# Two of 42 weight slabs multiplied without a split, and the finished output scattered without one, in the small slots of a mixture-of-experts kernel

## The chip, the cores and the metric

The kernel runs on one core of one Trainium2 chip. The metric is the device time of one execution in microseconds (us); smaller is better. The time before is the median of three runs.

## The reference

Two layers of a hybrid mixer with a residual each, the first followed by a dense SwiGLU, the second by a mixture of experts. Only the mixture of experts bears on the change:

```python
SEQ, D_MODEL, N_EXPERTS, TOP_K, D_FF_EXPERT = 256, 1024, 8, 2, 3584

def swiglu(h, w_gate_up, w_down):
    gt, up = jnp.split(h @ w_gate_up, 2, axis=-1)
    return (jax.nn.silu(gt) * up) @ w_down

def moe_swiglu(h, w_router, w_gate_up, w_down):
    t = h.reshape(-1, dm)                                   # 256 x 1024
    top_val, top_idx = lax.top_k(t @ w_router, TOP_K)
    combine = jnp.sum(jax.nn.one_hot(top_idx, N_EXPERTS) * jax.nn.softmax(top_val)[..., None], axis=1)
    y = jnp.zeros_like(t)
    for e in range(N_EXPERTS):
        y = y + combine[:, e:e + 1] * swiglu(t, w_gate_up[e], w_down[e])
    return y
```

All of it is float32: an expert has 1024 x 7168 weights for gate and up and 3584 x 1024 for down, 44 MB.

## The kernel before

**Split precision.** TensorE multiplies in a reduced form of float32 (`F32R`). So a matrix is split into a high part, `hi`, the operand rounded to `F32R`, and a low part, `lo = x - hi`. ScalarE writes the high part and VectorE the low part. A product is then three matmuls: hi x hi, hi x lo, lo x hi.

**Slots.** The expert stage works in slots `i`. A slot gathers up to 128 tokens of one expert (a full slot), or up to 64 (a small slot, `few`). Slots 2, 4 and 6 are small, all others full; eight slots, 0 to 7, are run with these inputs. In a small slot the stationary operand holds the high part of 64 tokens in its columns 0 to 63 and their low part in columns 64 to 127, so that two matmuls for each piece of weight, with `exp_hi` and with `exp_lo` (L2308, L2309), give all four terms. The rows of the low part are then added to the others by `fold_low`: ScalarE copies the product to `low_part` (L1163) and TensorE adds it through the matrix `fold`.

**Slabs.** Each slot streams the 44 MB of its expert from HBM in 42 slabs of 1 MB, 128 x 2048. SyncE issues their transfers (L572) into 14 buffers, `exp_slots`: slab `j` is asked for once TensorE has used slab `j - 14` (semaphore `slab_used`). ScalarE writes `exp_hi[:, place, :]` (L1121), a ring of `EXP_RING` = 6 places; VectorE writes the low part over the raw slab (L1671), since `exp_lo` and the raw buffers are the same memory. The function `ring_plan` says which place slab `j` takes and which slab, its `holder`, was there before. Both engines put their splits into their own program with `expert_split(i, few, used)`, called each time the program passes one more slab of TensorE's: it writes out further splits until

```python
place, holder = RINGS[few][j]
if holder >= used - LATE:        # LATE = 1
    return
```

so the number of splits that stand ahead of any other instruction of ScalarE or VectorE is fixed by the holders.

**A slot's order.** The hidden width 3584 is done in `STEPS` = 4 steps of 1024, 1024, 1024 and 512 columns. Step `s` makes the gate in PSUM bank pair 0 (`block(0, s, ..)`), the up product in pair 1 (`block(1, s, ..)`), and then the down product of the step before, `down(s - 1, ..)`. In slabs: step 0 has 0 to 7; step 1 has 8 to 11 (gate), 12 to 15 (up) and 16 to 19 (down); step 2 has 20 to 31 in the same way; step 3 has 32 and 33 (gate), 34 and 35 (up); then come 36 to 41 (down). ScalarE takes the silu of the gate (L1172), VectorE multiplies with the up product in `hidden(s)` (L1803), TensorE transposes the result in `turn_hidden(s)` (L2337), and ScalarE and VectorE split it (L1179, L1812).

**The two places.** In a small slot TensorE cannot begin slab 12, which overwrites bank pair 1, before `hidden(0)` has read that pair (place 1, behind slab 11); and it cannot run `turn_hidden(2)` before `hidden(2)` (place 2, behind slab 33).

**The finished output.** At the start of slot `i` the result of slot `i - 1` is copied from PSUM to `ysp[:, 0, :]` by ScalarE (L1190), its low part is made by VectorE in `output_lo` (L1770), and TensorE scatters both to the token rows by eight matmuls with the 0/1 matrix `selT` (`scatter`, L2075) behind slab 3. VectorE adds them to `xs` in `add_slot` (L1778).

Each engine runs its own program in order; semaphores alone connect them.

Of the kernel before, what the change touches and what calls it, by code (L numbers as in the profile page):

```python
# [22 lines left out]
F32 = mybir.dt.float32  # L23
# [34 lines left out]
EXP_RAW, EXP_RING, LATE = 14, 6, 1  # L58
# [12 lines left out]
EXP_SLABS = sum(2 * a + b for a, b in zip(GU, DN))  # L71
HT = DM // P
HT_END = STEP[-1][1] // P
assert EXP_SLABS % EXP_RAW == 0
UNSPLIT = ()


def ring_plan(few):

    plan, holders = [], [n - EXP_RING for n in range(EXP_RING)]  # L80
    for j in range(EXP_SLABS):
        if few and j in UNSPLIT:
            plan.append(None)
            continue
        place = sum(x is not None for x in plan) % EXP_RING
        plan.append((place, holders[place]))
        holders[place] = j
    assert holders == [EXP_SLABS - EXP_RING + n for n in range(EXP_RING)]
    return plan


RINGS = {few: ring_plan(few) for few in (False, True)}


def column(n):
# [98 lines left out]
def trunk(nc, x_in, mem_in, mix_norm_g, w_in, sb_q_g, sb_k_g, gla_a_up, gla_a_b, gla_o_g, ca_q_g,  # L194
# [5 lines left out]
    PRE = len(flat)  # L200
# [4 lines left out]
    with ExitStack() as ctx:  # L205
# [58 lines left out]
        exp_hi = sb("exp_hi", [P, EXP_RING, EXP_SLAB], F32R)  # L264
# [70 lines left out]
        count, key, rank, cap, few = (sm(240 + 8 * i, E) for i in range(5))  # L335
# [6 lines left out]
        pa = ctx.enter_context(nc.psum_tensor("pa", [P, 4 * BW], F32))  # L342
# [489 lines left out]
        def _(act):  # L832
# [277 lines left out]
            def expert_split(i, few, used, at_most=EXP_SLABS):  # L1110

                nonlocal j
                while j < at_most:
                    if RINGS[few][j] is not None:
                        place, holder = RINGS[few][j]
                        if holder >= used - LATE:
                            return
                        act.wait_ge(more_ready[j % EXP_RAW], i * (16 * EXP_SLABS // EXP_RAW)
                                    + 16 * (j // EXP_RAW + 1))
                        act.wait_ge(slab_used, i * EXP_SLABS + (PRE + holder + 1))  # L1120
                        act.activation(exp_hi[:, place, :], exp_slots[j % EXP_RAW], ACT.Copy)\  # L1121
                            .then_inc(hi_ready, counted(few, j))
                    j += 1
# [23 lines left out]
            def expert(i, few, next_few, folds=0):  # L1147
# [93 lines left out]
        def _(dve):  # L1241
# [541 lines left out]
            def expert(i, few, next_few, folds=0):  # L1783
# [111 lines left out]
        def _(pe):  # L1895
# [178 lines left out]
            def mm(dst, a, b, start, stop):  # L2074
                return pe.matmul(dst, a, b, start=start, stop=stop, skip_group_check=True)  # L2075
# [194 lines left out]
            def find_tokens(n):  # L2270
# [3 lines left out]
                    ins = mm(ps[:, DM:DM + 2], sel[:, t, :], token_no[:, t, :], t == 0, t == NT - 1)  # L2274
                ins.then_inc(token_found, 1)

            def scatter(n, halves=1):


                pe.wait_ge(selt_ready, n)  # L2280
                pe.wait_ge(y_lo, n + (halves - 1))
                for t in range(NT):
                    for c in range(2):
                        for h in range(2):
                            dst = (1 - t) * DM + c * BW
# [12 lines left out]

            def expert(i, few, folds=0):
                at = i * EXP_SLABS  # L2300
                j = 0

                def terms(dst, src, k, cols, first, last):

                    m_hi, m_lo = exp_hi[:, RINGS[few][j][0], cols], exp_lo[j % EXP_RAW][:, cols]
                    if not few:
                        return passes(dst, src[:, 0, k, :], src[:, 1, k, :], m_hi, m_lo, first, last)
                    pe.matmul(dst, src[:, 0, k, :], m_hi, start=first, stop=False)  # L2308
                    return pe.matmul(dst, src[:, 0, k, :], m_lo, start=False, stop=last)  # L2309
# [64 lines left out]
                for s in range(STEPS):  # L2374
# [81 lines left out]
```

## Time and profile before

| | us |
|---|---|
| median of 3 runs (1696.69 to 1698.57) | 1698.41 |
| the profiled execution's own time | 1697.4 |
| its span | 1695.5 |
| TensorE busy in the span | 1624.8 |
| VectorE busy | 1305.0 |
| ScalarE busy | 1107.4 |

The expert stage fills the second half. The copies L1190 that open slots 1 to 7 begin at 894.78, 1015.65, 1120.51, 1239.49, 1343.79, 1462.67 and 1567.64 us, and the last engine stops at 1695.5. Between two of these copies lies one slot. In the lists of this document an instruction stands with the time at which it begins, its duration, its engine, its line and operation, what it writes and what it reads; in square brackets stands how long the engine was idle before it, and what it waited for. TensorE's matmuls overlap in their pipeline: what a matmul takes away from the engine is the distance from its start to that of the next, not its duration, and the same holds to a smaller extent for VectorE and ScalarE.

### The profile page before, as it was taken

How to read it: one execution, taken by the hardware profiler on the slowest of the kernel's cores; microseconds unless marked ns; L12 is line 12 of the kernel's file. 1: busy time of each engine (PE TensorE's matmuls, PEld its weight loads, DVE VectorE, ACT ScalarE, POOL GpSimd, SP SyncE). 2: the span in 40 equal slices, each digit the busy share in tenths (PEclk: the TensorE clock that was granted, in tenths of full speed). 3: DMA queues.
4: the chain of work that ended last, by engine and by line, in shares of the span. 5: the costliest groups of instructions: out<-in, count | busy, mean ns of one | idle time of the engine just before them, and what ended most of it. 6: DMA issues, size and time to landing. Idle time of an engine off the chain costs nothing.

```text
span 1695.5 us, 20153 instructions
## 1 busy us (share of the span) xinstructions
PE 1624.8 (96%) x7598; PEld 1331.5 (79%) x7598; DVE 1305.0 (77%) x968; ACT 1107.4 (65%) x950; POOL 111.0 (7%) x123
## 2 busy tenths in 40 slices
PE   7999998999999999999999998899989899988998
PEld 5777886888887778877788887688877788876886
DVE  6654666555666546658989889999899998999985
ACT  5557554444555475546677778887689777887773
POOL 4111000000011110000400000000000000000000
PEclk9999999999999999999999999999999999999999
DMA  7554544656566544479999999999999999999990
GB/s 274 174 148 141 157 146 157 210 177 199 166 216 175 140 148 149 149 292 374 339 370 371 378 367 393 404 409 405 398 385 398 409 409 401 385 397 409 409 387 25
DMA packets 161335, 484.84 MB, mean 286 GB/s; under 512 B 12992, under 2 KB 15072, under 8 KB 161248
## 3 DMA queue, kind: packets, MB, share of 16 engines
q1 hardware_dynamic: 158112, 474.16, 76.9%
q0 software_dynamic: 3136, 9.48, 1.6%
q8 instruction: 60, 0.98, 0.2%
q14 instruction: 27, 0.22, 0.0%
HBM read 481.50 MB, written 2.10 MB: 285 GB/s over the span
## 4 chain that ended last, share of the span: by engine, by line
PE 81%; DVE 12%; issue 3%; ACT 2%; POOL 1%; DMA 0%; DVEq 0%; POOLq 0%; ACTq 0%
PE pa L1971 18%; PE pa L1973 17%; PE pa L1972 17%; DVE exp_lo_a L1671 5%; PE ps L2075 5%; PE ps L1971 4%; PE ps L1973 4%; PE ps L1972 4%; PE pa L2308 3%; PE pa L2309 3%; DVE exp_lo_b L1671 2%; PE ps L2337 1%; PE ps L2308 1%; PE ps L2309 1%; POOL hrs L712 1%
## 5 line engine op out<-in xcount | busy, mean ns | idle before, releaser
L1671 DVE TENSOR_TENSOR exp_lo_a<-exp_raw_a,exp_hi 128x2048 fp32r<-128x2048 f32 x240 | 538.4, 2288 | 28.9 <-ACT exp_hi L1121 28.5
L1121 ACT ACTIVATE exp_hi<-exp_raw_a 128x2048 fp32r<-128x2048 f32 x240 | 451.7, 1920 | 80.2 <-PE pa L1973 39.2
L1257 DVE TENSOR_TENSOR w_lo<-w_raw,w_hi 128x1024 fp32r<-128x1024 f32 (+1 forms) x228 | 277.2, 1231 | 136.2 <-ACT w_hi L846 127.1
L846 ACT ACTIVATE w_hi<-w_raw 128x1024 fp32r<-128x1024 f32 (+1 forms) x228 | 236.9, 1054 | 171.4 <-PE pa L1973 147.7
L1971 PE MATMUL pa<-w_hi,r 128*128 128x512 f32 x600 | 240.2, 400 | 0.0
L1973 PE MATMUL pa<-w_hi,r 128*128 128x512 f32 x600 | 234.2, 390 | 0.0
L1972 PE MATMUL pa<-w_lo,r 128*128 128x512 f32 x600 | 234.0, 390 | 0.0
L1671 DVE TENSOR_TENSOR exp_lo_b<-exp_raw_b,exp_hi 128x2048 fp32r<-128x2048 f32 x96 | 217.8, 2289 | 14.5 <-ACT exp_hi L1121 13.6
L1971 PE MATMUL pa<-exp_hi,xg 128*128 128x512 f32 x560 | 220.2, 393 | 2.5 <-ACT xg L1133 1.5
L1973 PE MATMUL pa<-exp_hi,xg 128*128 128x512 f32 x560 | 218.3, 390 | 0.0
L1121 ACT ACTIVATE exp_hi<-exp_raw_b 128x2048 fp32r<-128x2048 f32 x96 | 182.7, 1919 | 30.7 <-PE pa L1973 22.7
L2308 PE MATMUL pa<-exp_hi,xg 128*128 128x512 f32 x336 | 139.2, 414 | 14.3 <-issue 14.2
L1972 PE MATMUL pa<-exp_lo_a,xg 128*128 128x512 f32 x380 | 148.0, 389 | 0.0
L1971 PE MATMUL pa<-w_hi,xt 128*128 128x512 f32 (+1 forms) x320 | 124.5, 389 | 9.4 <-DVE xt L1293 9.4
L1971 PEld LDWEIGHTS pa<-w_hi,r 128*128 128x128 f32 x600 | 112.7, 188 | 25.5 <-issue 2.0
L1973 PEld LDWEIGHTS pa<-w_hi,r 128*128 128x128 f32 x600 | 112.7, 188 | 24.3
L1972 PEld LDWEIGHTS pa<-w_lo,r 128*128 128x128 f32 x600 | 112.8, 188 | 21.9
L1971 PEld LDWEIGHTS pa<-exp_hi,xg 128*128 128x128 f32 x560 | 105.2, 188 | 24.5 <-ACT xg L1133 1.6
L1973 PE MATMUL pa<-w_hi,xt 128*128 128x512 f32 (+1 forms) x320 | 122.9, 384 | 0.0
L1972 PE MATMUL pa<-w_lo,xt 128*128 128x512 f32 (+1 forms) x320 | 122.9, 384 | 0.0
L1973 PEld LDWEIGHTS pa<-exp_hi,xg 128*128 128x128 f32 x560 | 105.1, 188 | 22.1
L1971 PE MATMUL ps<-exp_hi,hts 128*128 128x512 f32 x240 | 94.5, 394 | 0.0
(301 smaller groups left out, 2270.2 us busy)
## 6 DMA issues: line engine op xcount, KB each, us to landing
exp_raw_a<-in_moe_w_gate_up SPq DMA_DIRECT2D x152, 1024.0 KB, 9.9
exp_raw_a<-in_moe_w_down SPq DMA_DIRECT2D x88, 1024.0 KB, 8.6
exp_raw_b<-in_moe_w_gate_up SPq DMA_DIRECT2D x72, 1024.0 KB, 9.2
w_raw<-in_w_in SPq DMA_DIRECT2D x104, 512.0 KB, 4.2
exp_raw_b<-in_moe_w_down SPq DMA_DIRECT2D x24, 1024.0 KB, 8.3
w_raw<-in_ff_w_gate_up SPq DMA_DIRECT2D x44, 512.0 KB, 4.5
w_raw<-in_ff_w_down SPq DMA_DIRECT2D x22, 512.0 KB, 3.9
w_raw<-in_w_mem_kv SPq DMA_DIRECT2D x16, 512.0 KB, 5.8
```

The costliest lines, as they stand in the source:

```text
L712: pool.tensor_tensor(dst[:, 0:n], src[:, 0:n], half[:, 0:n], ALU.pow)\
L846: act.activation(w_hi[:, s % SPLIT, 0:n], raw_slot(s)[:, 0:n], ACT.Copy)\
L1121: act.activation(exp_hi[:, place, :], exp_slots[j % EXP_RAW], ACT.Copy)\
L1257: dve.tensor_tensor(w_lo[:, s % SPLIT, 0:w], raw_slot(s)[:, 0:w], w_hi[:, s % SPLIT, 0:w].bitcast(F32), ALU.subtract)\
L1671: dve.tensor_tensor(exp_lo[j % EXP_RAW], exp_slots[j % EXP_RAW], exp_hi[:, place, :].bitcast(F32), ALU.subtract)\
L1971: pe.matmul(dst, hi, m_hi, start=first, stop=False)
L1972: pe.matmul(dst, hi, m_lo, start=False, stop=False)
L1973: return pe.matmul(dst, lo, m_hi, start=False, stop=last)
L2075: return pe.matmul(dst, a, b, start=start, stop=stop, skip_group_check=True)
L2308: pe.matmul(dst, src[:, 0, k, :], m_hi, start=first, stop=False)
L2309: return pe.matmul(dst, src[:, 0, k, :], m_lo, start=False, stop=last)
L2337: ins = pe.transpose(dst[:, a * P:(a + 1) * P], hs[:, a * P:(a + 1) * P], ident[:, :])
```

## The change

In small slots slabs 11 and 33 are no longer split. TensorE multiplies them from the raw buffer with full float32 operands, in four matmuls in place of eight, and waits for the transfer itself (`more_ready`). ScalarE and VectorE leave them out, and so the holders of the slabs behind them change: six slabs behind each of them have holder `j - 7` in place of `j - 6`. The places of the ring are turned by two after each small slot (`ring_of`). The output of the full slot before is copied to `y_whole`, in the memory of `hts`, and scattered by four full float32 matmuls in place of eight; VectorE's `output_lo` is left out at the start of small slots. Full slots keep their instructions.

```diff
-UNSPLIT = ()
+UNSPLIT = (11, 33)
-def ring_plan(few):
-    plan, holders = [], [n - EXP_RING for n in range(EXP_RING)]
+def ring_plan(few, offset):
+    plan, holders = [], [(n - offset) % EXP_RING - EXP_RING for n in range(EXP_RING)]
     for j in range(EXP_SLABS):
         if few and j in UNSPLIT:
             plan.append(None)
             continue
-        place = sum(x is not None for x in plan) % EXP_RING
+        place = (offset + sum(x is not None for x in plan)) % EXP_RING
         plan.append((place, holders[place]))
         holders[place] = j
+def ring_of(i, few):
+    smaller = (i - 1) // 2 if type(i) is int and i > 0 else 0
+    return ring_plan(few, -smaller * len(UNSPLIT) % EXP_RING)
...
                     act.wait_ge(slab_used, at + PRE)
-                    act.activation(ysp[:, 0, :], ps[:, 0:DM], ACT.Copy).then_inc(y_hi, 1)
+                    act.activation(y_whole[:, :] if few else ysp[:, 0, :], ps[:, 0:DM], ACT.Copy)\
+                        .then_inc(y_hi, 1)
...
                     expert_split(i, few, 0)
-                    output_lo(i)
+                    if few:
+                        dve.sem_inc(y_lo, 1)
+                    else:
+                        output_lo(i)
...
+            def scatter_whole(n):
+                pe.wait_ge(selt_ready, n)
+                pe.wait_ge(y_hi, n)
+                for t in range(NT):
+                    for c in range(2):
+                        dst = (1 - t) * DM + c * BW
+                        ins = mm(ps[:, dst:dst + BW], selT[:, t * P:(t + 1) * P].bitcast(F32),
+                                 y_whole[:, c * BW:(c + 1) * BW], True, True)
+                    ins.then_inc(scattered, 1)
...
-                        pe.wait_ge(lo_ready, at + (PRE + j + 1))
+                        if ring[j] is None:
+                            pe.wait_ge(more_ready[j % EXP_RAW], i * (16 * EXP_SLABS // EXP_RAW)
+                                       + 16 * (j // EXP_RAW + 1))
+                        else:
+                            pe.wait_ge(lo_ready, at + (PRE + j + 1))
...
+                                if ring[j] is None:
+                                    ins = pe.matmul(dst, xg[:, 0, k, :].bitcast(F32),
+                                                    exp_slots[j % EXP_RAW][:, cols],
+                                                    start=k == 0, stop=k == KT - 1)
+                                else:
+                                    ins = terms(dst, xg, k, cols, k == 0, k == KT - 1)
...
-                    if s == 0 and not is_first(i):
+                    if s == 0 and few:
+                        scatter_whole(i)
+                    elif s == 0 and not is_first(i):
                         scatter(i)
```

VectorE's program, from the start of small slot 2 to the split of the first hidden tile (L1812), before. L1770 is `output_lo`, L1778 `add_slot`, L1803 `hidden(0)`, L1671 the splits of slabs 5 to 18:

```order
L1770 TENSOR_TENSOR hts<-ps,hts 128x1024
L1671 TENSOR_TENSOR exp_lo_a<-exp_raw_a,exp_hi 128x2048 x2
L1671 TENSOR_TENSOR exp_lo_b<-exp_raw_b,exp_hi 128x2048
L1671 TENSOR_TENSOR exp_lo_a<-exp_raw_a,exp_hi 128x2048
L1778 SCALAR_TENSOR_TENSOR xs<-ps,small,xs 128x1024 x2
L1671 TENSOR_TENSOR exp_lo_a<-exp_raw_a,exp_hi 128x2048 x2
L1671 TENSOR_TENSOR exp_lo_b<-exp_raw_b,exp_hi 128x2048 x3
L1671 TENSOR_TENSOR exp_lo_a<-exp_raw_a,exp_hi 128x2048
L1803 TENSOR_TENSOR hs<-pa,hs 128x1024
L1819 TENSOR_SCALAR sel<-rev_tri,small 128x128 x2
L1671 TENSOR_TENSOR exp_lo_a<-exp_raw_a,exp_hi 128x2048 x4
L1812 TENSOR_TENSOR hts<-ps,hts 128x8x64
```

The same place now. The split is L1680, `add_slot` L1787, `hidden(0)` L1812, and the split of the hidden tile L1821; the first row holds the splits of slabs 0 to 6:

```order
L1680 TENSOR_TENSOR exp_lo_a<-exp_raw_a,exp_hi 128x2048 x7
L1680 TENSOR_TENSOR exp_lo_b<-exp_raw_b,exp_hi 128x2048
L1680 TENSOR_TENSOR exp_lo_a<-exp_raw_a,exp_hi 128x2048
L1787 SCALAR_TENSOR_TENSOR xs<-ps,small,xs 128x1024 x2
L1680 TENSOR_TENSOR exp_lo_a<-exp_raw_a,exp_hi 128x2048 x2
L1680 TENSOR_TENSOR exp_lo_b<-exp_raw_b,exp_hi 128x2048 x2
L1680 TENSOR_TENSOR exp_lo_a<-exp_raw_a,exp_hi 128x2048 x2
L1812 TENSOR_TENSOR hs<-pa,hs 128x1024
L1828 TENSOR_SCALAR sel<-rev_tri,small 128x128 x2
L1680 TENSOR_TENSOR exp_lo_a<-exp_raw_a,exp_hi 128x2048 x3
L1821 TENSOR_TENSOR hts<-ps,hts 128x8x64
```

`output_lo` is gone. Between `add_slot` and `hidden(0)` stand six splits before and now: slab 11 is missing, and slab 15 has moved ahead of `hidden(0)` in its stead. Behind `hidden(0)` three splits stand where four stood.

VectorE's program around `hidden(2)`, before. The first rows are eight splits, ending with slab 36; the last two rows of L1671 are slabs 37 and 38, then 39 and 40:

```order
L1671 TENSOR_TENSOR exp_lo_a<-exp_raw_a,exp_hi 128x2048 x6
L1671 TENSOR_TENSOR exp_lo_b<-exp_raw_b,exp_hi 128x2048
L1671 TENSOR_TENSOR exp_lo_a<-exp_raw_a,exp_hi 128x2048
L1803 TENSOR_TENSOR hs<-pa,hs 128x1024
L1671 TENSOR_TENSOR exp_lo_a<-exp_raw_a,exp_hi 128x2048 x2
L1812 TENSOR_TENSOR hts<-ps,hts 128x8x64
L1671 TENSOR_TENSOR exp_lo_b<-exp_raw_b,exp_hi 128x2048 x2
L1803 TENSOR_TENSOR hs<-pa,hs 128x512
```

The same place now; `hidden(2)` is the first L1812:

```order
L1680 TENSOR_TENSOR exp_lo_a<-exp_raw_a,exp_hi 128x2048 x5
L1680 TENSOR_TENSOR exp_lo_b<-exp_raw_b,exp_hi 128x2048
L1680 TENSOR_TENSOR exp_lo_a<-exp_raw_a,exp_hi 128x2048 x2
L1812 TENSOR_TENSOR hs<-pa,hs 128x1024
L1680 TENSOR_TENSOR exp_lo_a<-exp_raw_a,exp_hi 128x2048
L1680 TENSOR_TENSOR exp_lo_b<-exp_raw_b,exp_hi 128x2048
L1821 TENSOR_TENSOR hts<-ps,hts 128x8x64
L1680 TENSOR_TENSOR exp_lo_b<-exp_raw_b,exp_hi 128x2048
L1812 TENSOR_TENSOR hs<-pa,hs 128x512
```

Eight splits stand ahead of `hidden(2)` before and now: slab 33 is missing and slab 37 has moved ahead. One split fewer stands between the split of the hidden tile and `hidden(3)`.

TensorE's program at place 2, now: the last pair of slab 32, slab 33 from the raw buffer, `turn_hidden(2)`, and slab 34.

```order
L2332 MATMUL pa<-exp_hi,xg 128x512
L2333 MATMUL pa<-exp_lo_a,xg 128x512
L2351 MATMUL pa<-exp_raw_a,xg 128x512 x4
L2371 MATMUL ps<-ident,hs 128x128 x8
L2332 MATMUL pa<-exp_hi,xg 128x512
```

Before, four pairs of L2308 and L2309 stood where the four matmuls L2351 stand; the rest of the order is the same.

## Rows read from the trace of the kernel before

**Rows 1.** All engines' busy time in slots 2, 3, 4 and 6 (us).

```profile
core 0: us, PE busy (x) PEld busy (x) DVE busy (x) ACT busy (x) POOL busy (x), PEclk, DMA share, GB/s
...
1015.60:1120.50 104.90, 94.26 (x411) 76.14 (x410) 102.81 (x58) 89.97 (x61) 0.99 (x1) 0.93 1.02 401
1120.50:1239.50 119.00, 119.00 (x547) 98.86 (x546) 108.09 (x58) 87.67 (x55) 2.21 (x1) 1.00 1.02 397
1239.50:1343.80 104.30, 93.65 (x410) 75.71 (x409) 102.59 (x58) 89.97 (x62) 0.99 (x1) 0.95 1.02 402
...
1462.70:1567.60 104.90, 94.32 (x410) 76.19 (x409) 102.72 (x58) 89.91 (x61) 0.99 (x1) 0.93 1.02 403
```

**Rows 2.** TensorE in slot 2, in order of time.

```profile
1039.95 0.39 PE L2309 MATMUL pa<-exp_lo_b,xg 128*128 128x512 f32 x1
1045.08 0.76 PE L2308 MATMUL pa<-exp_hi,xg 128*128 128x512 f32 x1 [4.73 <-issue]
...
1090.07 0.39 PE L2308 MATMUL pa<-exp_hi,xg 128*128 128x512 f32 x1
1090.29 0.39 PE L2309 MATMUL pa<-exp_lo_a,xg 128*128 128x512 f32 x1
...
1098.45 1.97 PE L2337 MATMUL ps<-ident,hs 128*128 128x128 f32 x8 [5.61 <-DVE hs L1803]
```

**Rows 3.** VectorE in slot 2, in order of time.

```profile
1018.23 1.22 DVE L1770 TENSOR_TENSOR hts<-ps,hts 128x1024 fp32r<-128x1024 f32 x1
1019.36 4.48 DVE L1671 TENSOR_TENSOR exp_lo_a<-exp_raw_a,exp_hi 128x2048 fp32r<-128x2048 f32 x2
...
1041.56 2.28 DVE L1671 TENSOR_TENSOR exp_lo_a<-exp_raw_a,exp_hi 128x2048 fp32r<-128x2048 f32 x1
1043.76 1.22 DVE L1803 TENSOR_TENSOR hs<-pa,hs 128x1024 f32<-128x1024 f32 x1
...
1054.09 0.68 DVE L1812 TENSOR_TENSOR hts<-ps,hts 128x512 fp32r<-128x512 f32 x1
1055.62 4.49 DVE L1671 TENSOR_TENSOR exp_lo_a<-exp_raw_a,exp_hi 128x2048 fp32r<-128x2048 f32 x2 [0.85 <-ACT exp_hi L1121]
...
1097.17 1.23 DVE L1803 TENSOR_TENSOR hs<-pa,hs 128x1024 f32<-128x1024 f32 x1
```

**Rows 4.** Busy time in stretches of slots 2, 4 and 6; columns as in rows 1.

```profile
1015.60:1040.30 24.70, 24.70 (x111) 20.12 (x109) 24.70 (x14) 24.36 (x17) 0.00 (x0) 1.00 1.02 407
1040.30:1045.10 4.80, 0.07 (x2) 0.05 (x1) 4.80 (x5) 4.23 (x3) 0.00 (x0) 0.72 1.03 410
1045.10:1052.00 6.90, 6.90 (x27) 5.61 (x27) 6.90 (x6) 1.92 (x1) 0.00 (x0) 0.70 1.02 398
1052.00:1092.80 40.80, 40.49 (x181) 31.91 (x179) 39.92 (x22) 40.52 (x27) 0.99 (x1) 1.00 1.02 391
1092.80:1098.50 5.70, 0.10 (x2) 0.05 (x1) 5.70 (x5) 1.65 (x2) 0.00 (x0) 0.87 1.02 408
1098.50:1120.50 22.00, 22.00 (x96) 18.41 (x97) 20.79 (x13) 17.29 (x13) 0.00 (x0) 0.88 1.03 409
1323.00:1343.80 20.80, 20.80 (x96) 17.56 (x97) 20.63 (x13) 17.31 (x14) 0.00 (x0) 0.94 1.03 409
1545.60:1567.60 22.00, 22.00 (x96) 18.40 (x97) 20.76 (x13) 17.26 (x13) 0.00 (x0) 0.88 1.03 409
```

**Rows 5.** TensorE: eight full float32 matmuls of 256 columns (16 records), in order of time.

```profile
218.90 3.62 PE L2075 MATMUL ps<-ckT,cqT 128*128 128x256 f32 x16
222.16 0.58 PE L1971 MATMUL pa<-w_hi,r 128*128 128x512 f32 x1
```

**Rows 6.** ScalarE in slot 2, in order of time.

```profile
1053.68 3.72 ACT L1121 ACTIVATE exp_hi<-exp_raw_a 128x2048 fp32r<-128x2048 f32 x2
```

**Rows 7.** Transfer of slab 38: issue, us to landing, and ScalarE's splits 37 and 38.

```profile
1074.83 0.98 SPq L572 DMA_DIRECT2D exp_raw_a<-in_moe_w_down  x1
...
exp_raw_a<-in_moe_w_down SPq DMA_DIRECT2D x1, 1024.0 KB, 14.7
...
1090.21 3.75 ACT L1121 ACTIVATE exp_hi<-exp_raw_a 128x2048 fp32r<-128x2048 f32 x2
```

More of the change, by code:

```diff
@@ L84, in ring_plan @@
             continue
-        place = sum(x is not None for x in plan) % EXP_RING
+        place = (offset + sum(x is not None for x in plan)) % EXP_RING
         plan.append((place, holders[place]))
         holders[place] = j
-    assert holders == [EXP_SLABS - EXP_RING + n for n in range(EXP_RING)]
+    assert sorted(holders) == [EXP_SLABS - EXP_RING + n for n in range(EXP_RING)]
     return plan
-RINGS = {few: ring_plan(few) for few in (False, True)}
+def ring_of(i, few):
+    smaller = (i - 1) // 2 if type(i) is int and i > 0 else 0
+    return ring_plan(few, -smaller * len(UNSPLIT) % EXP_RING)
+assert 3 * len(UNSPLIT) % EXP_RING == 0 and EXP_SLABS % EXP_RING == 0
 def column(n):
@@ L103, in counted @@
 def counted(few, j):
-    return 2 if j + 1 < EXP_SLABS and RINGS[few][j + 1] is None else 1
+    return 2 if few and j + 1 in UNSPLIT else 1
 CAP, FEW = P, P // 2
@@ L270, in trunk @@
         with nc.sbuf_tensor("route_x", [P, NT, KT, P], F32) as route_x:
+            pass
+        with nc.sbuf_tensor("y_whole", [P, DM], F32) as y_whole:
             pass
@@ L1113, in expert_split @@
                 while j < at_most:
-                    if RINGS[few][j] is not None:
-                        place, holder = RINGS[few][j]
+                    if ring_of(i, few)[j] is not None:
+                        place, holder = ring_of(i, few)[j]
                         if holder >= used - LATE:
@@ L1665, in expert_split @@
                 while j < at_most:
-                    if RINGS[few][j] is not None:
-                        place, holder = RINGS[few][j]
+                    if ring_of(i, few)[j] is not None:
+                        place, holder = ring_of(i, few)[j]
                         if holder >= used - LATE:
@@ L2300, in expert @@
                 at = i * EXP_SLABS
+                ring = ring_of(i, few)
                 j = 0
                 def terms(dst, src, k, cols, first, last):
-                    m_hi, m_lo = exp_hi[:, RINGS[few][j][0], cols], exp_lo[j % EXP_RAW][:, cols]
+                    m_hi, m_lo = exp_hi[:, ring[j][0], cols], exp_lo[j % EXP_RAW][:, cols]
                     if not few:
@@ L2319, in block @@
                             for c in range(0, w, BW):
-                                ins = terms(pa[:, bank * DM + c:bank * DM + c + BW], xg, k,
-                                            slice(kk * w + c, kk * w + c + BW), k == 0, k == KT - 1)
+                                dst = pa[:, bank * DM + c:bank * DM + c + BW]
+                                cols = slice(kk * w + c, kk * w + c + BW)
+                                if ring[j] is None:
[4 more added lines that the diff above has]
+                                    ins = terms(dst, xg, k, cols, k == 0, k == KT - 1)
                         ins.then_inc(slab_used, 1)
```

## The prediction

> **What bounds the kernel now.** I read three views in turn: the engines' busy time slot by slot, TensorE in order of time inside a small slot, and VectorE beside it.
>
> The first [rows 1] separates the slots. In full slot 3 TensorE is busy for 119.00 of 119.00 us: it is the bound, and the change leaves its work there alone. In small slots 2, 4 and 6 TensorE has 94 us of work in 104.9, 104.3 and 104.9 us, while VectorE is busy for 102.8. The clock column shows 0.93 to 0.95 there against 1.00. The transfers move 397 to 403 GB/s in slots of both kinds, with a share of 1.02: they too have hardly anything to spare.
>
> TensorE's list shows where it stops [rows 2]. It issues the last matmul of slab 11 at 1039.95 and the next at 1045.08, after 4.73 us (place 1); the end of that wait has no releaser in the profile ("issue"), but `hidden(0)` ends at 1043.76 + 1.22 = 1044.98 [rows 3]. It stops again for 5.61 us until 1098.45, by name for VectorE's L1803, `hidden(2)` (place 2). Everything else is close: in 1015.6 to 1040.3 TensorE is busy for all 24.70 us, and from 1098.5 to the slot's end for all 22.00, with the next full slot behind it [rows 1, 4]. VectorE is busy for 24.70 of 24.70 and 4.80 of 4.80 us before place 1, and its one gap up to place 2 that I find is 0.85 us at 1055.62, where it waits for ScalarE's split [rows 3, 4].
>
> So a small slot is a relay: TensorE runs to place 1, VectorE decides when it goes on; VectorE decides again at place 2; from there to the end of the next full slot TensorE runs without a stop. **What a small slot saves is the time by which `hidden(2)` ends sooner, plus what TensorE's clock gains behind it.** Work taken off VectorE behind `hidden(2)` is worth nothing.
>
> The clock matters. During the wait at place 1 the granted clock falls from 1.00 (2.4 GHz) towards 0.5 (1.2 GHz), and in the 6.9 us behind it the mean is 0.70: 0.30 x 6.9 = 2.07 us lost. Behind place 2 the means are 0.88 over 22.0 us, 0.94 over 20.8 and 0.88 over 22.0 in the three small slots: 2.64, 1.25 and 2.64 us lost, 6.5 in all [rows 4].
>
> **The change, part by part, in slot 2.**
>
> *VectorE, `output_lo`.* L1770 begins at 1018.23 and the next split at 1019.36: 1.13 us go [rows 3]. VectorE does not pause from there to `hidden(0)`, so `hidden(0)` comes 1.13 us sooner.
>
> *VectorE, slab 11.* A split takes 1043.76 - 1041.56 = 2.20 us of the engine [rows 3]. The order printed above decides where this counts: ahead of `hidden(0)` stand as many splits as before, slab 15 in place of 11. Nothing is saved at place 1. Behind `hidden(0)` there is one fewer: 2.20 us sooner from L1812 on.
>
> *VectorE, slab 33.* Again as many splits, eight, stand ahead of `hidden(2)`; the one saved lies behind it, where TensorE is the bound. Worth 0; should TensorE not be the bound there, it would be 2.20 us.
>
> *TensorE, full precision.* No row shows a full float32 matmul with 512 columns. The nearest has 256: eight of them take 222.16 - 218.90 = 3.26 us, 0.41 us each [rows 5], so 0.82 for 512 and 3.3 us for four. The other end is four times a reduced matmul: 111 matmuls in 24.70 us are 0.225 us each [rows 4], hence 0.90 and 3.6 us. Eight reduced ones are 1.8 us. Each of the three replacements (scatter, slab 11, slab 33) therefore costs TensorE 1.5 us, at most 1.8. I take 1.5, since its row has the same kind of operand. The Trainium skill, "FP8 and Floating Point Precision", section "TensorE Precision Notes", has true FP32 as four passes through the array; by it the price would be the upper end, 1.8 us (the row of 256 columns shows 3.6 times a reduced matmul, a little less), and the forecast the same, for the reason that follows.
>
> *TensorE at place 1.* It would have been able to go on at 1039.95 + 0.225 = 1040.18; with 1.5 for the scatter and 1.5 for slab 11 that is 1043.2 (1043.8 by the upper end). `hidden(0)` lets it go at 1045.08 - 1.13 = 1043.95. So the extra work lies in the wait, of which 0.1 to 0.8 us stays. In 1052.0 to 1092.8 TensorE also pauses, for 0.31 us in all, and the clock stays at 1.00 [rows 4], so I take 1.00 behind place 1, and the 2.07 us come back: at what was 1052.0, TensorE is 1.13 + 2.07 = 3.2 us ahead. If the clock falls all the same, it is 1.13.
>
> *VectorE behind place 1.* By its own work it is 1.13 + 2.20 = 3.33 us ahead at L1812, and it has the gap of 0.85 us behind it. That gap ends with ScalarE's split of slab 19, which starts at 1053.68 [rows 6] behind the copy of TensorE's transposes, so it moves with TensorE, 3.2 us. Hence the next splits, and 41.5 us on, `hidden(2)`, come 3.2 us sooner. VectorE is busy for 39.92 of 40.8 us in that stretch [rows 4], and the same instructions stand in it.
>
> *TensorE at place 2.* Slab 32 ended at 1090.29 + 0.23 = 1090.5 and now ends at 1087.3, since it is paced by VectorE's splits. Slab 33 takes 3.3 us instead of 1.8 and needs no split: ready at 1090.6. `hidden(2)` lets it go at 1098.45 - 3.2 = 1095.25. TensorE still waits some 4.6 us, as long as at place 1 before, where the clock fell. So I leave the clock's loss behind place 2 as it is.
>
> *ScalarE* loses two splits and gains nothing; it waits for TensorE, not the reverse. *Other costs.* TensorE's wait for a transfer is met long before: slab 38, the tightest that I found, landed at 1074.83 + 14.7 = 1089.5, with ScalarE's split of it, the second of a pair from 1090.21, beginning near 1092.0 [rows 7].
>
> **Sum.** 3.2 us for each of three small slots: 9.6. Full slots 0. From the profiled execution's own 1697.4 that is 1687.8. The median of the runs lies 1.0 above that execution, so I predict **1688.8 us**.
>
> **The rivals.**
>
> *A. The clock holds at place 2.* The wait shrinks from 5.6 to 4.6 us, and where and how far the clock falls varies between slots already (0.94 against 0.88). If it stayed at 1.00 in all three, 6.5 us more would come back: 9.6 + 6.5 = 16.1, 1682.3 us. Against it: waits of 4.7 us at place 1 did bring it down [rows 4]. The other way, if it falls as long after the last matmul and for as long as now, 1.0 us less of the slow stretch lies in the wait: 0.5 us more is lost in each slot, and 1.4 more if slot 4 becomes like the others: 2.9 us less, 1691.7. The Trainium skill, "TensorE: Matmul & The Clock Gate", section "HAM oscillation — how this bites in real kernels", warns that waits of PE can make the clock fall anew each time round a loop; the rows of both places agree, and by it place 2 keeps its loss, as forecast.
>
> *B. The transfers become the bound.* A slab of 1.049 MB at 409 GB/s [rows 4] takes 2.56 us, 42 take 107.7, more than a small slot lasts; small and full slot together have 223.9 us for 215.4. After the change 220.7 are left, which still holds. But slab 38 had only 2.5 us to spare, less than 3.2: ScalarE would wait 0.7 us there. VectorE reaches that slab behind `hidden(2)`, so this is hidden. If the lag piles up from slot to slot, the later two small slots win nothing: 3.2 in all, 1695.2 us.
>
> *C. Slower: full precision costs more than the wait at place 1.* With x us for a full float32 matmul TensorE reaches place 1 at 1040.18 - 3.6 + 8x. Since the clock would not have fallen, it is later than before only beyond 1045.08 + 2.07 = 1047.15, x = 1.32. With 0.82 to 0.90 there is 3.4 us of room. It is passed if these matmuls run at half clock: x = 1.64 to 1.8 gives 1049.7 to 1051, 2.5 to 3.8 us later than before in each slot, 1706 to 1710 us. Against it: the clock is 1.00 up to place 1, and nothing ahead of it stops TensorE.
>
> *D. Place 1's clock still falls.* TensorE would gain only 1.13 us there and reach `turn_hidden(0)` that late, VectorE's gap would grow by 2.1 us, and the slot would save 1.1: 3.4 in all, 1695.0 us.
>
> **How the numbers follow.** Forecast 0.62, A's better half 0.16, B 0.08, D 0.08, C 0.06. A measurement of this kernel can tell about 0.2%, 3.4 us. The forecast and A are faster by more; B and D, at 3.2 to 3.4, stand at the border, half of them in each; the forecast's own tail and part of C give the rest. Faster 0.85, within 0.2% 0.10, slower 0.05. The likeliest case alone spans 1686 to 1691.7; with A below and B and D above I give 1682.5 to 1695.2.
>
> **What would show it.** Right: L1190 to L1190 in small slots near 101.5 us, full slots still 119; TensorE's wait at place 1 under 1 us with clock 1.00 behind it; the wait at place 2 near 4.6 us; each full-precision slab 3.3 to 3.6 us. Wrong: a `hidden(2)` that is not 3.2 us sooner (then a gap of VectorE ahead of it shows which engine it waits for), a small slot's last stretch shorter than 21 us at clock 1.00 (A), ScalarE waiting for transfers (B), or four matmuls of a raw slab above 5.3 us (C).

## The result, and the profile after

| | before | after |
|---|---|---|
| median of 5 runs (us) | 1697.39 (1696.69 to 1698.57) | 1687.55 (1686.59 to 1688.85) |
| ratio, 95% interval | | 0.994 (0.9927 to 0.9953) |
| profiled execution, its span | 1697.4, 1695.5 | 1686.59, 1684.8 |

The kernel became 9.8 us faster; 9.6 was forecast. The forecast time, 1688.8 us, holds 1.0 us that was added because the median of the first three runs lay above the profiled execution; over the five runs it does not (1697.39 against 1697.4). The copies that open slots 2 to 7 now begin at 1014.34, 1115.51, 1234.48, 1336.59, 1455.49 and 1556.44 us. The busy time of slots 2, 3, 4 and 6, and of the stretches behind the two places (columns as in rows 1; they answer to [rows 1, 4]):

```profile
1014.30:1115.50 101.20, 95.94 (x411) 74.07 (x410) 97.32 (x55) 86.99 (x59) 0.99 (x1) 0.98 1.02 401
1115.50:1234.50 119.00, 119.00 (x547) 98.85 (x546) 108.13 (x58) 87.67 (x55) 2.22 (x1) 1.00 1.03 406
1234.50:1336.60 102.10, 96.89 (x410) 74.86 (x409) 97.32 (x55) 87.07 (x60) 0.99 (x1) 0.97 1.03 405
1455.50:1556.40 100.90, 95.67 (x410) 73.94 (x409) 97.25 (x55) 86.91 (x59) 0.99 (x1) 0.98 1.02 402
...
1042.90:1049.80 6.90, 6.87 (x34) 5.82 (x35) 6.90 (x6) 3.95 (x5) 0.00 (x0) 1.00 1.02 407
1094.40:1115.50 21.10, 21.10 (x96) 17.70 (x97) 18.58 (x12) 15.49 (x12) 0.00 (x0) 0.92 1.03 409
1315.50:1336.60 21.10, 21.10 (x93) 17.53 (x92) 17.63 (x12) 15.52 (x13) 0.00 (x0) 0.89 1.03 409
1535.50:1556.40 20.90, 20.86 (x96) 17.61 (x97) 18.63 (x12) 15.46 (x12) 0.00 (x0) 0.93 1.03 409
```

The full slot is as long as before, 119.0 us. The small slots went from 104.9, 104.3 and 104.9 to 101.2, 102.1 and 100.9. Behind place 1 the clock is 1.00 where it was 0.70. Behind place 2 it still falls.

TensorE in slot 2, in order of time (answers to [rows 2]): the scatter, slab 11, the restart at place 1, slab 33, the restart at place 2.

```profile
1021.39 3.60 PE L2087 MATMUL ps<-y_whole,selT 128*128 128x512 f32 x8
1024.42 0.79 PE L2332 MATMUL pa<-exp_hi,xg 128*128 128x512 f32 x1
...
1038.69 3.59 PE L2351 MATMUL pa<-exp_raw_b,xg 128*128 128x512 f32 x8
1042.93 0.47 PE L2332 MATMUL pa<-exp_hi,xg 128*128 128x512 f32 x1 [0.65 <-issue]
...
1047.14 1.04 PE L2371 MATMUL ps<-ident,hs 128*128 128x128 f32 x8
...
1086.45 3.59 PE L2351 MATMUL pa<-exp_raw_a,xg 128*128 128x512 f32 x8
1094.39 1.72 PE L2371 MATMUL ps<-ident,hs 128*128 128x128 f32 x8 [4.34 <-DVE hs L1812]
```

The wait at place 1 shrank from 4.73 to 0.65 us, that at place 2 from 5.61 to 4.34. Four full float32 matmuls stand as eight records and last 3.6 us from first start to last end; one of their records is 0.59 us long, 0.2 more than one of a reduced matmul.

VectorE in slot 2 (answers to [rows 3]):

```profile
1017.20 4.50 DVE L1680 TENSOR_TENSOR exp_lo_a<-exp_raw_a,exp_hi 128x2048 fp32r<-128x2048 f32 x2 [0.21 <-ACT exp_hi L1129]
...
1041.61 1.22 DVE L1812 TENSOR_TENSOR hs<-pa,hs 128x1024 f32<-128x1024 f32 x1
...
1049.74 0.69 DVE L1821 TENSOR_TENSOR hts<-ps,hts 128x512 fp32r<-128x512 f32 x1
1051.56 4.49 DVE L1680 TENSOR_TENSOR exp_lo_a<-exp_raw_a,exp_hi 128x2048 fp32r<-128x2048 f32 x2 [1.13 <-ACT exp_hi L1129]
...
1093.10 1.23 DVE L1812 TENSOR_TENSOR hs<-pa,hs 128x1024 f32<-128x1024 f32 x1
...
1101.63 2.29 DVE L1680 TENSOR_TENSOR exp_lo_b<-exp_raw_b,exp_hi 128x2048 fp32r<-128x2048 f32 x1 [2.30 <-ACT exp_hi L1129]
```

Counted from the slot's opening copy, `hidden(0)` begins at 27.27 us instead of 28.11, and `hidden(2)` at 78.76 instead of 81.52. What VectorE saves with slab 33 stands behind that, as a gap of 2.30 us.

ScalarE now waits for transfers, which it did nowhere in the small slots before; in slot 2 (waits: us in total, times, longest):

```profile
ACT exp_hi L1129 <- DMA exp_raw_a<-in_moe_w_down: 1.9, 3, 0.7
...
ACT exp_hi L1129 <- DMA exp_raw_b<-in_moe_w_down: 0.6, 1, 0.6
```

In slots 4 and 6 the sums are 3.0 and 2.3 us.

### The profile page after: what moved, and what is told of

Same layout as the page of the kernel before. It is cut to its first block, busy times and chain, and to the rows that moved or that the text cites. A ratio compares the mean times of both kernels' runs of the same rounds, so it can differ in the third digit from the quotient of the medians.

```text
span 1684.8 us, 20141 instructions
## 1 busy us (share of the span) xinstructions
PE 1630.4 (97%) x7598; PEld 1325.4 (79%) x7598; DVE 1288.8 (76%) x959; ACT 1098.4 (65%) x944; POOL 111.0 (7%) x123
## 3 DMA queue, kind: packets, MB, share of 16 engines
q0 software_dynamic: 3136, 9.48, 1.6%
## 4 chain that ended last, share of the span: by engine, by line
PE 82%; DVE 12%; ACT 2%; issue 2%; POOL 1%; DMA 0%; DVEq 0%; POOLq 0%; ACTq 0%
PE pa L1983 18%; PE pa L1985 18%; PE pa L1984 18%; DVE exp_lo_a L1680 5%; PE ps L2087 5%; PE ps L1983 4%; PE ps L1985 4%; PE ps L1984 4%; PE pa L2332 3%; PE pa L2333 3%; DVE exp_lo_b L1680 2%; PE ps L2371 1%; PE ps L2332 1%; PE ps L2333 1%; POOL hrs L720 1%
## 5 line engine op out<-in xcount | busy, mean ns | idle before, releaser
L1680 DVE TENSOR_TENSOR exp_lo_a<-exp_raw_a,exp_hi 128x2048 fp32r<-128x2048 f32 x237 | 531.7, 2287 | 29.6 <-ACT exp_hi L1129 29.2
L1129 ACT ACTIVATE exp_hi<-exp_raw_a 128x2048 fp32r<-128x2048 f32 x237 | 446.5, 1918 | 82.8 <-PE pa L1985 39.3
L1680 DVE TENSOR_TENSOR exp_lo_b<-exp_raw_b,exp_hi 128x2048 fp32r<-128x2048 f32 x93 | 211.2, 2288 | 20.2 <-ACT exp_hi L1129 19.5
L1983 PE MATMUL pa<-exp_hi,xg 128*128 128x512 f32 x560 | 220.2, 393 | 2.4 <-ACT xg L1141 1.5
L1985 PE MATMUL pa<-exp_hi,xg 128*128 128x512 f32 x560 | 218.3, 390 | 0.0
L1129 ACT ACTIVATE exp_hi<-exp_raw_b 128x2048 fp32r<-128x2048 f32 x93 | 176.7, 1917 | 33.3 <-PE pa L1985 22.8
L2332 PE MATMUL pa<-exp_hi,xg 128*128 128x512 f32 x312 | 126.4, 405 | 2.0 <-issue 2.0
```

The costliest lines, as they stand in the source:

```text
L1983: pe.matmul(dst, hi, m_hi, start=first, stop=False)
L1985: return pe.matmul(dst, lo, m_hi, start=False, stop=last)
```

## The experiments

The theories: **relay** (a microsecond counts if it makes `hidden(2)` come sooner, and what the clock gains counts), **work** (each microsecond taken off VectorE counts, since it is busy for 98% of a small slot), **clock** (the whole gain is the clock at place 1), **waits** (an unsplit slab pays only where TensorE waits). Each small slot is told in two numbers, from the opening copy to the start of `hidden(2)`, and from there to the next opening copy:

| kernel | to `hidden(2)`, slots 2, 4, 6 | rest, slots 2, 4, 6 | median us | ratio to before |
|---|---|---|---|---|
| before | 81.52, 82.20, 81.58 | 23.34, 22.10, 23.38 | 1697.39 | |
| after | 78.76, 78.74, 78.78 | 22.41, 23.36, 22.16 | 1687.55 | 0.994 (0.9927, 0.9953) |
| output unsplit alone | 80.37, 80.26, 79.63 | 23.41, 23.09, 23.23 | 1691.32 | 0.9967 (0.9955, 0.9979) |
| slab 11 alone | 81.20, 79.61, 79.62 | 23.26, 23.31, 23.30 | 1692.86 | 0.9974 (0.9963, 0.9984) |
| slab 33 alone | 81.10, 82.10, 82.37 | 23.10, 23.67, 22.17 | 1697.22 | 1.0 (0.9991, 1.0009) |
| both but for slab 33 | 78.76, 78.77, 78.77 | 22.62, 23.33, 22.12 | 1687.47 | 0.9944 (0.993, 0.9957) |
| after, again | 78.75, 78.77, 78.77 | 22.93, 23.54, 22.28 | 1687.87 | 0.9943 (0.993, 0.9957) |
| slabs 11 and 27 | 76.55, 76.57, 77.61 | 22.07, 22.43, 23.30 | 1680.53 | 0.9906 (0.9891, 0.9921) |
| after, place 2 filled | 78.77, 78.77, 78.77 | 21.02, 21.03, 21.04 | 1683.26 | 0.9916 (0.9902, 0.9929) |
| before, place 1 filled | 80.46, 80.48, 80.46 | 23.35, 22.93, 22.75 | 1692.75 | 0.9976 (0.9967, 0.9986) |
| before, both filled | 80.47, 80.47, 80.46 | 21.27, 21.27, 21.26 | 1687.92 | 0.9945 (0.9931, 0.9958) |
| 11 and 27, place 2 filled | 76.57, 76.57, 79.25 | 21.27, 23.14, 23.98 | 1680.20 | 0.9901 (0.9886, 0.9916) |
| slabs 11, 22 and 27 | 75.29, 76.65, 80.12 | 21.27, 23.26, 23.33 | 1680.37 | 0.9899 (0.9884, 0.9914) |

The ratios are to a kernel before that was timed beside the experiments: 1697.21 us for the first four, 1696.88 for the next four, 1697.49 for the last three.

The rest is counted to the next copy, which is ScalarE's. In most rows that copy begins 2.2 us after TensorE's first matmul of the full slot. It begins later in slot 6 of "slabs 11 and 27" (3.2 us), in slots 4 and 6 of "11 and 27, place 2 filled" (4.1 and 3.8) and of "slabs 11, 22 and 27" (4.2 and 2.9), so those five numbers are too long for what TensorE does, by 0.7 to 2.0 us.

### The parts apart

The output unsplit, no slab unsplit. (In all kernels of this section `ring_of` also gives the offset of the last slot's loop, which matters only with one or three unsplit slabs.)

```diff
-UNSPLIT = (11, 33)
+UNSPLIT = ()
```

> The kernel before with one part of the change: the finished output is scattered unsplit in small slots, and no slab is left unsplit. Relay theory (only what makes hidden(2) come sooner counts, plus the granted clock): hidden(0) comes 0.8 us sooner, TensorE still waits some 2.5 us at place 1; if the clock still falls there, a small slot is 0.8 us shorter (2.5 us in all), if it stays at 1.00 up to 1.7 us shorter (5 us in all). Work theory (every microsecond taken off VectorE counts): 3 x 1.13 = 3.4 us. Clock theory (the whole gain is the clock at place 1): 6 us or nothing.

It gained 5.9 us (interval 3.6 to 7.6), and 5.0 by the sum of the three `hidden(2)`: 1.15, 1.94 and 1.95. The work theory's 3.4 us are just outside the interval; the clock theory's 6 are inside. The slots tell them apart: the wait at place 1 was 2.28 us, and behind it the clock stayed at 1.00 in slot 6 but fell in slots 2 and 4 (a mean of 0.83 over ten microseconds), and these gained all the same. My upper end of 1.7 us a slot was too low. It took VectorE's gap ahead of slab 19 from slot 2, 0.85 us; in slot 6 of the kernel before it is 0.92, and in slot 4:

```profile
1280.14 2.29 DVE L1671 TENSOR_TENSOR exp_lo_a<-exp_raw_a,exp_hi 128x2048 fp32r<-128x2048 f32 x1 [1.52 <-ACT exp_hi L1121]
```

Slab 11 alone, with `output_lo`, `ysp` and the split scatter of the kernel before:

```diff
-UNSPLIT = (11, 33)
+UNSPLIT = (11,)
...
-                    if few:
-                        dve.sem_inc(y_lo, 1)
-                    else:
-                        output_lo(i)
+                    output_lo(i)
```

> Slab 11 alone is left unsplit. Relay theory: hidden(0) does not move, the wait at place 1 shrinks from 4.7 to 3.1 us. If the clock still falls, VectorE's saved 2.2 us turn into a longer gap ahead of slab 19, since that gap ends with TensorE, and nothing is gained (0 us); if the clock holds, up to 2.1 us for each small slot (6.2 in all). Work theory: 6.6 us either way.

This run holds both cases. TensorE in slot 2, at the restart at place 1:

```profile
1044.96 0.55 PE L2328 MATMUL pa<-exp_hi,xg 128*128 128x512 f32 x1 [3.12 <-issue]
1045.31 0.63 PE L2329 MATMUL pa<-exp_lo_b,xg 128*128 128x512 f32 x1
1045.73 0.63 PE L2328 MATMUL pa<-exp_hi,xg 128*128 128x512 f32 x1
```

A matmul each 0.42 us, in place of 0.225, is the slow clock. VectorE's gap ahead of slab 19 grew to 1.74 us in that slot, with another of 0.90 ahead of it:

```profile
1050.54 2.29 DVE L1679 TENSOR_TENSOR exp_lo_a<-exp_raw_a,exp_hi 128x2048 fp32r<-128x2048 f32 x1 [0.90 <-ACT exp_hi L1129]
...
1055.18 4.49 DVE L1679 TENSOR_TENSOR exp_lo_a<-exp_raw_a,exp_hi 128x2048 fp32r<-128x2048 f32 x2 [1.74 <-ACT exp_hi L1129]
```

So 2.2 us of VectorE's work were saved, and `hidden(2)` came 0.3 us sooner. In slots 4 and 6 the clock stayed at 1.00 after the same wait of 3.1 us, and `hidden(2)` came 2.6 and 2.0 sooner. The work theory's 6.6 us are outside the interval (2.7 to 6.3 us).

Slab 33 alone, again with `output_lo`, `ysp` and the split scatter:

```diff
-UNSPLIT = (11, 33)
+UNSPLIT = (33,)
```

> Slab 33 alone is left unsplit. Relay theory: its split is saved behind hidden(2), so nothing is gained (0 us), but for a clock that may fall otherwise behind place 2, where the wait shrinks from 5.6 to 4.0 us (3 us either way in all). Work theory: 6.6 us faster than before.

No gain, within 0.1%, with 4.3 us of wait left at place 2. VectorE in slot 2, `hidden(2)` and then the gap in which the saved split went:

```profile
1095.06 1.22 DVE L1811 TENSOR_TENSOR hs<-pa,hs 128x1024 f32<-128x1024 f32 x1
...
1104.26 2.29 DVE L1679 TENSOR_TENSOR exp_lo_b<-exp_raw_b,exp_hi 128x2048 fp32r<-128x2048 f32 x1 [2.98 <-ACT exp_hi L1129]
```

The change without slab 33:

```diff
-UNSPLIT = (11, 33)
+UNSPLIT = (11,)
```

> The change without slab 33: slab 11 unsplit and the output scattered unsplit. Relay theory: the same time as the full change within 2 us, 1686 to 1690 us, with hidden(2) as soon. Work theory: 6.6 us slower than the full change, 1694 us.

The same time as the change, and `hidden(2)` at the same 78.77. Slab 33, one of the two unsplit slabs, adds nothing that these runs can measure.

### The slab moved, and the clock by itself

> The changed kernel once more, beside the next three on the same chip: 1687.5 us, 0.994 of the kernel before.

As expected; beside it the kernel before took 1696.88 us, 9.0 more. The rest behind `hidden(2)` is 68.75 us over the three slots, 68.82 before. In the first profile of the change it was 67.93: these 0.9 us did not come again, while the 9.0 us ahead of `hidden(2)` did.

Slab 27, the last up slab of step 2, in the place of slab 33:

```diff
-UNSPLIT = (11, 33)
+UNSPLIT = (11, 27)
```

> The change with slab 27 left unsplit in the place of slab 33: as much work for every engine, but seven splits in the place of eight stand ahead of hidden(2). Relay theory: hidden(2) comes 2.2 us sooner in each small slot, 6.6 us in all, 1681 us, less what ScalarE then waits for transfers. Work theory: the same as the change, 1687.5 us. Waits theory (an unsplit slab pays only where TensorE waits): slower than the change, since TensorE's 1.5 us for slab 27 lie in no wait.

`hidden(2)` in slot 2, and the three small slots:

```profile
1091.49 1.21 DVE L1812 TENSOR_TENSOR hs<-pa,hs 128x1024 f32<-128x1024 f32 x1
```

```profile
1014.90:1113.60 98.70, 94.73 (x411) 74.33 (x410) 97.17 (x55) 86.92 (x60) 0.99 (x1) 0.98 1.03 404
1232.50:1331.50 99.00, 95.03 (x410) 74.46 (x409) 97.30 (x55) 87.22 (x60) 0.99 (x1) 0.98 1.03 406
1450.40:1551.40 101.00, 96.00 (x415) 75.29 (x415) 98.66 (x55) 87.56 (x60) 0.99 (x1) 0.98 1.03 407
```

With VectorE's work unchanged (97.2 and 97.3 us in slots 2 and 4, as after the change) `hidden(2)` comes 2.2 us sooner in slots 2 and 4 and 1.2 in slot 6, and the kernel is 7.3 us faster than the change. That rules out the work and the waits theory, which gave no gain and a loss. In slot 6 VectorE had two more gaps ahead of `hidden(2)`, of 0.36 and 0.28 us, behind a ScalarE that waited for landings. A transfer issued there at 1495.34, for slab 33, took 20.6 us to land (14.7 for slab 38 of slot 2 before):

```profile
exp_raw_a<-in_moe_w_gate_up SPq DMA_DIRECT2D x1, 1024.0 KB, 20.6
```

Matmuls that nothing reads, at place 2 of the change:

```diff
+            def keep_busy(n):
+                for _ in range(n):
+                    mm(ps[:, DM + BW:2 * DM], xg[:, 0, 0, :],
+                       xg[:, 0, 0:4, :].rearrange("p k c -> p (k c)"), True, True)
...
                     if s > (1 if few else 0):
+                        if few and s == 3:
+                            keep_busy(18)
                         turn_hidden(s - 1)
```

> The change with 18 matmuls of 512 columns at place 2 whose product nothing reads (4.05 us in a wait of 4.3). If the clock behind place 2 is lost through the wait, it stays at 1.00 and the 1.7, 2.3 and 1.5 us that it costs in the three small slots come back: 5.5 us, 1682 us. If it is not, 1687.5 us.

TensorE in slot 2, and the stretch behind the restart with its slot:

```profile
1092.04 4.69 PE L2087 MATMUL ps<-xg 128*128 128x512 f32 x18
1096.88 0.88 PE L2376 MATMUL ps<-ident,hs 128*128 128x128 f32 x6 [0.15 <-DVE hs L1812]
```

```profile
1016.80:1116.60 99.80, 98.71 (x429) 76.03 (x428) 97.36 (x55) 86.90 (x59) 0.99 (x1) 1.00 1.03 404
...
1095.60:1116.60 21.00, 20.83 (x101) 16.86 (x101) 19.93 (x14) 15.57 (x12) 0.00 (x0) 1.00 1.02 408
```

All three small slots are 99.8 us long, with a rest of 21.0 in place of 22.2 to 23.5. The clock's price behind place 2 is 4.6 us by the medians (1687.87 - 1683.26), and 5.7 by the rests of the two profiled executions (68.75 - 63.09); 5.5 were expected.

The same in the kernel before, at place 1 alone:

```diff
                     if s == 1:
                         pe.wait_ge(selt_ready, i + 1)
+                        if few:
+                            keep_busy(20)
```

> The kernel before, with nothing of the change, and 20 matmuls of 512 columns at place 1 whose product nothing reads (4.5 us in a wait of 4.7). Clock theory: TensorE's 2.07 us come back in each small slot and are the most of the change's gain: 6 us faster than before. Relay theory: VectorE's own work sets hidden(2), so only its gap of 0.85 us can close: at most 2.5 us faster. Work theory: 0.

It gained 4.1 us without any work taken away. VectorE in slot 2: no gap is left ahead of slab 19, and `hidden(2)`:

```profile
1053.07 0.68 DVE L1820 TENSOR_TENSOR hts<-ps,hts 128x512 fp32r<-128x512 f32 x1
1053.67 4.48 DVE L1679 TENSOR_TENSOR exp_lo_a<-exp_raw_a,exp_hi 128x2048 fp32r<-128x2048 f32 x2
...
1095.10 1.21 DVE L1811 TENSOR_TENSOR hs<-pa,hs 128x1024 f32<-128x1024 f32 x1
```

`hidden(2)` came 1.1, 1.7 and 1.1 us sooner, 3.9 in all. I had said at most 2.5, with the gap of slot 2 for all three. The gaps are 0.85, 1.52 and 0.92, and closing each gave 0.2 us more than it shows. The gain is less than the clock theory's 6 (interval 2.4 to 5.6): once its gap is closed, VectorE's own work is the limit.

And with 23 more at place 2:

```diff
+                        if few and s == 3:
+                            keep_busy(23)
                         turn_hidden(s - 1)
```

> The kernel before with nothing of the change, and matmuls whose product nothing reads in both waits: 20 at place 1, 23 at place 2. Relay theory with the clock: hidden(2) begins 80.5 us after the slot's start, as with the matmuls at place 1 alone, and the rest of the slot takes 21.0 us at clock 1.00: small slots of 101.5 us, 9.6 us faster than before in all, 1687.5 us, as much as the change. Work theory: no change.

```profile
1014.50:1116.30 101.80, 100.10 (x453) 80.59 (x453) 101.80 (x57) 89.99 (x62) 0.99 (x1) 1.00 1.03 405
1235.20:1336.90 101.70, 99.99 (x453) 80.53 (x452) 101.70 (x57) 89.98 (x61) 0.99 (x1) 1.00 1.03 405
1455.80:1557.50 101.70, 100.04 (x453) 80.48 (x453) 101.70 (x57) 89.87 (x61) 0.99 (x1) 1.00 1.03 404
```

Filling both waits of the kernel before with useless matmuls is worth as much as the change, 0.9945 against 0.9943. The shares differ: `hidden(2)` is 1.7 us later than with the change, the rest 0.9 to 2.3 us shorter. VectorE is busy for all of the slot's 101.7 us.

The rest is 21.27 us and not the 21.0 expected, and here slab 33 does show. VectorE and TensorE in slot 2, `hidden(3)` and the transposes behind it:

```profile
1105.54 0.68 DVE L1811 TENSOR_TENSOR hs<-pa,hs 128x512 f32<-128x512 f32 x1
...
1106.28 0.66 PE L2372 MATMUL pa<-ident,hs 128*128 128x128 f32 x4
```

TensorE's matmul ahead of these transposes began at 1105.86, 0.42 us before them in place of 0.225, so it waits 0.2 us for `hidden(3)`, which begins 10.54 us behind `hidden(2)`. With slab 33 unsplit and place 2 filled it begins 9.48 us behind, TensorE does not wait, and the rest is 21.02. So with a clock of 1.00 behind place 2 the split of slab 33 costs about 0.25 us a slot; where the clock fell, it cost nothing that was measured. No run changed this slab alone at a held clock.

### Where it ends

The two best parts together, with 13 matmuls at place 2, and a third unsplit slab:

```diff
-UNSPLIT = (11, 33)
+UNSPLIT = (11, 27)
...
+                            keep_busy(13)
```

> Slabs 11 and 27 unsplit, and 13 matmuls whose product nothing reads in the 3.3 us wait at place 2. If the parts add up: small slots of 97.6 us, 1676 us. Transfers: small and full slot together then last 216.6 us, and 84 slabs of 2.56 us need 215.4 before the gathers; ScalarE waits for its slabs in slots 4 and 6 and VectorE with it, so only slot 2 reaches 97.6 and the time ends at 1677 to 1680 us.

```diff
-UNSPLIT = (11, 33)
+UNSPLIT = (11, 22, 27)
```

> A third unsplit slab, 22, ahead of hidden(2). Relay theory without transfers: hidden(2) 2.2 us sooner once more, TensorE arrives at place 2 with about 1 us of wait left, the clock stays at 1.00, small slots of 95.5 us, 1671 us. Transfers as the bound: slot 2 alone gets shorter; in slots 4 and 6 VectorE stands behind ScalarE's wait for landings, and the time stays within 2 us of the kernel with slabs 11 and 27, 1679 to 1682 us.

Both end where slabs 11 and 27 alone end, 1680.2 and 1680.4 us against 1680.5; for the first that is just above the 1677 to 1680 expected, for the second within the range. The third slab's small slots, and what ScalarE waited for in its slot 6:

```profile
1014.60:1111.20 96.60, 95.49 (x411) 72.98 (x410) 94.39 (x53) 85.06 (x58) 0.99 (x1) 1.00 1.03 404
1230.10:1330.00 99.90, 97.41 (x419) 74.59 (x418) 96.76 (x54) 85.87 (x59) 0.99 (x1) 1.00 1.03 406
1446.90:1550.30 103.40, 97.68 (x413) 75.13 (x412) 96.54 (x54) 85.86 (x58) 0.99 (x1) 0.97 1.03 407
```

```profile
ACT exp_hi L1129 <- DMA exp_raw_a<-in_moe_w_down: 7.9, 7, 4.1
...
ACT exp_hi L1129 <- DMA exp_raw_a<-in_moe_w_gate_up: 1.4, 2, 0.8
```

From copy to copy the small slots are 96.6, 99.9 and 103.4 us, but the copy that ends slot 4 is late. TensorE's first matmul of slot 5, the split of ScalarE that stands ahead of the copy, and the copy:

```profile
1325.79 0.39 PE L1983 MATMUL pa<-exp_hi,xg 128*128 128x512 f32 x1
...
1328.16 1.92 ACT L1129 ACTIVATE exp_hi<-exp_raw_a 128x2048 fp32r<-128x2048 f32 x1 [0.65 <-DMA exp_raw_a<-in_moe_w_gate_up]
1329.98 1.01 ACT L1198 ACTIVATE hts<-ps 128x1024 fp32r<-128x1024 f32 x1
```

ScalarE stands 4.2 us behind TensorE there, in place of 2.2, since it waits for landings; from copy to copy the full slot behind is then 116.9 us, for 119. Counted from TensorE's first matmul of one slot to that of the next, the small slots are:

| kernel | slot 2 | slot 4 | slot 6 | sum |
|---|---|---|---|---|
| slabs 11 and 27 | 96.62 | 97.00 | 97.87 | 291.5 |
| 11 and 27, place 2 filled | 95.84 | 95.84 | 99.64 | 291.3 |
| slabs 11, 22 and 27 | 94.55 | 95.92 | 100.75 | 291.2 |

So slots 2 and 4 both keep their gain, also in the second kernel, of which I had expected it of slot 2 alone, and slot 6 gives all of it back. In slot 6 ScalarE waits 9.3 and 10.1 us for landings in the last two kernels, VectorE has five and nine gaps of 0.3 to 1.4 us behind it ahead of `hidden(2)`, and `hidden(2)` comes at 79.25 and 80.12. That the transfers are the bound is read from these waits; no run gave them more room.

## Why the prediction was right

**What sets a small slot.** Right. Only time ahead of `hidden(2)` and the clock counted: slab 33 is worth nothing (alone 1.0, left out of the change 0.9944 against 0.9943), and 2.2 us a slot, until the transfers interfere, as soon as its like stands ahead of `hidden(2)`.

**`output_lo`, 1.13 us.** Mis-sized: 0.84 (28.11 to 27.27). VectorE arrives earlier at the split of slab 5 and waits there for ScalarE (0.21 us at 1017.20), which makes the high part of that slab behind the copy of the finished output. The working said that VectorE does not pause up to `hidden(0)`; before, it did not, and the cover was thin.

**Slab 11, no gain at place 1 and 2.20 us behind it.** Right: `hidden(0)` moved by `output_lo` alone, and VectorE's split of the hidden tile came at 1049.74 - 1014.34 = 35.40 us instead of 38.44, 3.04 sooner, 0.84 + 2.20.

**Full precision.** 1.5 us were taken for each replacement, 1.8 the upper end. The scatter cost 1.6: slab 11 begins 1038.69 - 1014.34 = 24.35 us behind the opening copy, and 22.72 before, where its first matmul was

```profile
1038.37 0.39 PE L2308 MATMUL pa<-exp_hi,xg 128*128 128x512 f32 x1
```

The wait at place 1 fell by 4.08 us, of which 0.84 are `hidden(0)`; the 3.24 left for scatter and slab 11 together agree. The 0.65 us that remain are within the 0.1 to 0.8 of the working.

**The clock at place 1.** Right, 1.00 for 0.70. From the restart to the transposes L2371 TensorE takes 1047.14 - 1042.93 = 4.21 us, and took 1051.21 - 1045.08 = 6.13 before:

```profile
1051.21 1.03 PE L2337 MATMUL ps<-ident,hs 128*128 128x128 f32 x8
```

So 1.92 us came back, for the 2.07 forecast. Alone, the clock at place 1 was worth 4.1 us in the three slots; without it slab 11 saved 0.3 us in a slot instead of 2.0 to 2.6. Neither half of the 3.2 us stands without the other: VectorE has to be early and TensorE has to feed ScalarE's copy early.

**`hidden(2)` 3.2 us sooner in each slot.** 2.76, 3.46 and 2.80: 9.0 of the 9.6. Slot 2's 2.76 is 0.84 + 1.92, TensorE's path; VectorE was 3.04 ahead by its own work, and the difference is the longer gap, 1.13 for 0.85. Slot 4 gained more than slot 2, since its gap had been 1.52: taking slot 2 for all three made up for a part of the two terms that were too large. That the measured 9.8 lies so near 9.6 is luck as well: the mechanism accounts for 9.0, and the second measurement gave 9.0.

**Place 2.** A wait of 4.34 us for the forecast 4.6, and a clock that falls as before. Rival A did not come about in the change; forced, it gave 4.6 us by the medians, 5.7 by the slots, where 5.5 were expected from the clock column (1.7, 2.3 and 1.5). Rival B was there but hidden: one wait of ScalarE of 0.7 us was worked out, and there were four of 0.6 to 0.7, 2.5 us in slot 2, none of which held VectorE up ahead of `hidden(2)`. About 7 us further down the time stops falling, with these waits grown to 9.3 us and more in slot 6.

## What to carry to other kernels

Where two engines hand work to each other, find the instruction whose end releases the other, and count only what stands ahead of it in its own engine's order. Work taken off the busier engine behind that instruction was worth nothing here while the clock fell, and the planner's look-ahead (here the ring, which drew slab 37 ahead of `hidden(2)` for the missing slab 33) can undo a saving ahead of it. Where TensorE waits, look at the clock column behind the wait: before any restructuring, a few matmuls that nothing reads show what the clock costs.

## What the runs showed of the hardware

How much of a wait TensorE's clock bears was not the same from slot to slot. At place 1, after waits of 4.7 us, it fell from 2.4 towards 1.2 GHz in all six small slots of the kernel before and of slab 33 alone; after 3.1 us in one of three; after 2.3 us in two of three; after 0.65 us in none. At place 2 it fell in every slot with a wait of 3.3 us or more, and after 2.0 us (slot 6 of "11 and 27, place 2 filled"), but not after 1.8 us (slot 4 of "slabs 11, 22 and 27"). Where both waits of a small slot were down to 0.65 us or less, the clock was 1.00 throughout. In the change with place 2 filled and in the kernel before with both filled this made the three slots equally long to 0.02 us, where they had differed by 1.2 and 0.7.

A full float32 matmul of 512 columns took 0.86 us of TensorE, a reduced one 0.225: the four of the scatter took the 1.81 us of the eight reduced ones and 1.63 more.
